# A halved Fourier transform in a transformer pair on one core, and twelve instead of four output-weight chunks loaded among the gate tiles

## The reference

```
sh1, sc1, g1, sh2, sc2, g2 = split(silu(c) @ w_mod + b_mod, 6)
h = rms_norm(x, norm_g[0]) * (1 + sc1) + sh1
hg = h.reshape(B, 256, 8, 256)                       # 8 groups of 256 features
y = real(fftn(hg, axes=(tokens, features in a group))).reshape(B, 256, 2048) @ fnet_w_out
x = x + g1 * rms_norm(y, norm_g[1])
x = x + g2 * rms_norm(relu2(modulate(rms_norm(x, norm_g[2]), sh2, sc2) @ w_mlp_in) @ w_mlp_out, norm_g[3])
```

## Time and profile before

| | |
|---|---|
| median of 3 runs | 2141.73 us (2141.72 to 2143.09) |
| the profiled execution | 2140.67 us, of which 2138.7 us is the span from the first to the last instruction |
| TensorE busy | 2096.8 us, 98% |
| VectorE busy | 1316.0 us, 62% |
| ScalarE busy | 985.5 us, 46% |
| mean granted TensorE clock | 0.997 |
| output product (f0 to f31) on TensorE | 172.69 to 264.92 us |
| start of the second half of the first MLP pair on TensorE | 321.24 us |

### The profile page before, as it was taken

How to read it: one execution, slowest core, us unless ns; L and a number is a source line. 1 busy time by engine, 2 the same in 40 slices (tenths; PEclk the granted TensorE clock), 3 DMA queues, 4 the chain that set the end, 5 groups by cost and what they waited for, 6 DMA issues and landing times.

```text
span 2138.7 us, 30220 instructions
## 1 busy us (share of the span) xinstructions
PE 2096.8 (98%) x11177; PEld 1764.5 (83%) x11177; DVE 1316.0 (62%) x1310; ACT 985.5 (46%) x1261; POOL 46.5 (2%) x71
## 2 busy tenths in 40 slices
PE   6899999999999999999999999999999999999999
PEld 3767878888888888887988888888888888888887
DVE  3878987656655655656767476555645655554553
ACT  4344355444344443434555567553434434343442
POOL 0010000000000000001100000000000000000000
PEclk9999999999999999999999999999999999999999
DMA  9999997677667667666665555566566656656654
GB/s 388 383 394 395 389 391 213 213 222 210 211 221 208 216 213 219 210 211 215 198 179 158 155 158 181 193 182 191 189 196 187 190 193 189 190 190 194 188 191 154
DMA packets 219374, 479.52 MB, mean 224 GB/s; under 512 B 14764, under 2 KB 15144, under 8 KB 218520
## 3 DMA queue, kind: packets, MB, share of 16 engines
q1 hardware_dynamic: 211956, 450.98, 65.1%
q0 software_dynamic: 6656, 26.21, 3.9%
q10 hardware_dynamic: 676, 1.14, 0.1%
HBM read 473.02 MB, written 5.25 MB: 224 GB/s over the span
## 4 chain that ended last, share of the span: by engine, by line
PE 89%; DVE 4%; DMA 3%; ACT 2%; issue 1%; SPq 1%; DVEq 0%; ACTq 0%
PE ps L537 46%; PE ps L499 21%; PE ps L504 11%; DVE acc L1552 2%; DMA raw<-in_w_mod_dram 1%; PE ps L521 1%; PE ps L523 1%; PE ps L522 1%; DMA raw<-in_w_mem_kv_dram 1%; PE ps L586 1%; PE ps L795 1%; PE ps L793 1%; PE ps L794 1%; PE ps L909 1%; PE ps L625 1%
## 5 line engine op out<-in xcount | busy, mean ns | idle before, releaser
L1527 DVE TENSOR_TENSOR wl<-raw,wh 128x1024 fp32r<-128x1024 f32 x684 | 808.2, 1222 | 314.1 <-ACT wh L1082 313.0
L1082 ACT ACTIVATE wh<-raw 128x1024 fp32r<-128x1024 f32 x684 | 696.7, 1054 | 522.4 <-DMA raw<-in_w_down_dram 161.9
L499 PE MATMUL ps<-xt,wh 128*128 128x512 f32 x1984 | 623.4, 395 | 1.6 <-DVE xt L1766 0.8
L537 PE MATMUL ps<-wh,u 128*128 128x512 f32 x2176 | 584.7, 389 | 1.0 <-DVE u L2052 0.6
L537 PEld LDWEIGHTS ps<-wh,u 128*128 128x128 f32 x2176 | 407.4, 188 | 85.8 <-DVE u L2052 1.0
L504 PEld LDWEIGHTS ps<-xt,wl 128*128 128x128 f32 x1984 | 372.7, 188 | 88.0
L504 PE MATMUL ps<-xt,wl 128*128 128x256 f32 x1984 | 389.7, 278 | 0.0
L537 PE MATMUL ps<-wl,u 128*128 128x512 f32 x1088 | 335.2, 389 | 0.0
L499 PEld LDWEIGHTS ps<-xt,wh 128*128 128x128 f32 x1984 | 302.5, 189 | 4.0 <-issue 2.5
L537 PE MATMUL ps<-wh,xt 128*128 128x512 f32 x960 | 269.1, 394 | 4.1 <-DVE wl L1527 2.8
L537 PEld LDWEIGHTS ps<-wl,u 128*128 128x128 f32 x1088 | 204.2, 188 | 42.4
(11 more groups left out here) (298 smaller groups left out, 1383.2 us busy)
## 6 DMA issues: line engine op xcount, KB each, us to landing
raw<-in_w_mod_dram SPq DMA_DIRECT2D x144, 512.0 KB, 9.8
raw<-in_w_mlp_in_dram SPq DMA_DIRECT2D x128, 512.0 KB, 3.8
raw<-in_w_mlp_out_dram SPq DMA_DIRECT2D x128, 512.0 KB, 4.8
raw<-in_w_up_dram SPq DMA_DIRECT2D x128, 512.0 KB, 3.8
raw<-in_w_down_dram SPq DMA_DIRECT2D x128, 512.0 KB, 3.7
raw<-in_w_in_dram SPq DMA_DIRECT2D x96, 512.0 KB, 3.8
slot<-in_w_mod_dram POOLq DMA_DIRECT2D x32, 512.0 KB, 5.2
raw<-in_w_out_dram SPq DMA_DIRECT2D x32, 512.0 KB, 3.7
```

The source lines that it names most:

```text
L499: mm(ps[:, 4 * par + j, :], wh[:, at, t, j * P:(j + 1) * P], flat(xt[:, kt, :, :]), start=kt == 0, stop=kt == KT - 1, skip_group_check=True)
L537: last = mm(o, act[:, kt, z, half * P:(half + 1) * P], w, start=kt == 0 and n == 0, stop=kt == KT - 1 and n == 2, skip_group_check=True)
L1082: A(flat(wh[:, i, :, :]), tile_at(landed[0]), ACT.Copy).then_inc(sem("w_hi"), 1)
L1527: V.tensor_tensor(flat(low_at(s)), tile_at(s), flat(wh[:, i, :, :]).bitcast(F32), ALU.subtract).then_inc(sem("w_lo"), 1)
```

## The change

The token transform of real data is symmetric in frequency, so half of the frequencies suffice. `dft_tokens` now makes `NF + 1` = 130 columns of the cosine and as many of the sine part (260 in all), and 129 of each are kept. `dft_features(q)` takes two groups at once, with 2 x 129 columns of cosine and 2 x 127 of sine sums, into separate column ranges of a bank, in 24 matmuls for each pair and 96 in all. The parts are then joined: ScalarE copies the two edge frequencies and the sine sums to `praw` (`fm_parts`), VectorE writes the difference and, in reversed order, the sum (`fm_sum`), and `fm_hi` and `fm_lo` split a pair's 1024 elements. The first two pairs' operands are prepared ahead of the first feature matmul. `G1_ROWS_AT` puts the rows of g1 tiles 8, 12 and 16 behind pairs 1, 2 and 3; those of tiles 20 to 23 come after the last pair, ahead of f0, and those of tiles 24 to 27 after f3. VectorE sums tiles 6 and 7 after the third pair's operands.

`AHEAD` goes from 4 to 12. On SyncE, 20 g1 tiles are alone, the last twelve alternate with f0 to f11, f12 to f31 have an sc2 tile each behind them, and twelve sc2 tiles follow f31. VectorE makes the low parts of f0 to f11 without sc2 sums beside them and has twelve of these sums after f31. `gate_rows` moves from behind f4 to behind f9, and the two halves of the gate to f12 and f13, the first output block to f14. All the slots from g1 tile 21 on move with the order, since they are counted from it.

```diff
-AHEAD = 4
+AHEAD = 12
...
-                            last = mm(o, xn[:, z, half, d0:d0 + P], t[:, half, :], start=half == 0 and z == 0 and t is dfth,
+                            last = mm(o, xn[:, z, half, d0:d0 + P], freqs(t[:, half, :])[:, :, 0:NF + 1], start=half == 0 and z == 0 and t is dfth,
...
+            def dft_features(q):
+                pe.wait_ge(sem("p_lo"), q + 1)
+                if q >= 2:
+                    pe.wait_ge(sem("fm_sum"), q - 1)
                 for dq in range(2):
+                    o = ps[:, pair_bank(q) + dq, :]
                     for kt in range(2):
                         for part in range(2):
                             lhs = slice(part * S + dq * P, part * S + (dq + 1) * P)
+                            cols = slice(2 * NF, 2 * S) if part else slice(0, 2 * NF)
+                            start = kt == 0 and part == 0
+                            mm(o[:, cols], dfth[:, kt, lhs], pdft[:, q % 2, kt, 0, cols], start=start, stop=False, skip_group_check=True)
+                            mm(o[:, cols], dftl[:, kt, lhs], pdft[:, q % 2, kt, 0, cols], start=False, stop=False, skip_group_check=True)
+                            last = mm(o[:, cols], dfth[:, kt, lhs], pdft[:, q % 2, kt, 1, cols], start=False,
...
-            for g in range(8):
-                dft_features(g)
-                if g in G1_ROWS_AT:
-                    n = G1_ROWS_AT[g]
+            for q in range(PAIRS):
+                dft_features(q)
+                for n in G1_ROWS_AT[q]:
                     if n == KT:
                         pe.wait_ge(sem("tok_out"), 8)
                     mod_rows("g1", C_G1, n, 2 if n < KT else 4)
             pe.wait_ge(sem("rows_folded"), 5)
+            mod_rows("g1", C_G1, 20, 4)
...
                     N_chunk(G_FN + g, i, xt, False, *early(CH * (G_FN + g) + i), fn_bank(g))
-                    if (g, i) == (0, 4):
+                    if (g, i) == (0, 3):
+                        mod_rows("g1", C_G1, 24, 4)
+                    if (g, i) == (1, 1):
                         pe.wait_ge(sem("rows_folded"), 6)
                         pe.wait_ge(sem("mod_out"), 2)
                         gate_rows(0, (4, 5, 6, 7))
...
+            def fm_parts(q):
+                act.wait_ge(sem("dft_d"), q + 1)
+                A(fm(q)[:, :, :, 0:NF:NF - 1], even_sums(q, slice(0, NF, NF - 1)), ACT.Copy)
+                A(fmq(q), ps[:, pair_bank(q):pair_bank(q) + 2, 2 * NF:2 * S].rearrange("p d (g n) -> p g d n", g=2),
+                  ACT.Copy).then_inc(sem("fm_part"), 1)
+            def fm_hi(q):
+                act.wait_ge(sem("fm_sum"), q + 1)
+                A(turned_rows(q, 0), fm(q), ACT.Copy).then_inc(sem("fm_hi"), 1)
...
+            def fm_sum(q):
+                dve.wait_ge(sem("fm_part"), q + 1)
+                t = fm(q)
+                V.tensor_tensor(t[:, :, :, 1:NF - 1], even_sums(q, slice(1, NF - 1)), fmq(q), ALU.subtract)
+                V.tensor_tensor(t[:, :, :, S - 1:NF - 1:-1], even_sums(q, slice(1, NF - 1)), fmq(q),
+                                ALU.add).then_inc(sem("fm_sum"), 1)
...
-                    if g == 0 and i < AHEAD:
+                    if CH * g + i < AHEAD:
                         continue
                     lo_static(CH * G + i)
                     gemv("sc2", C_FN, CH * g + i - AHEAD, 1)
-                    if (g, i) in ((0, 6), (1, 1)):
-                        gate(0, (4, 6), 0, (g,))
-                    if g and i == 3:
+                    if (g, i) in ((1, 4), (1, 5)):
+                        gate(0, (4, 6), 0, (i - 4,))
+                    if g and i == (3 if g > 1 else 6):
                         y_block(g - 1)
...
-G1_ROWS_AT = {1: 8, 2: 12, 3: 16, 4: 20, 5: 24}
-G1_AT = [(6, 7), (), (), (), (), (), (), ()]
+G1_ROWS_AT = [(), (8,), (12,), (16,)]
+G1_AT = [(6, 7), (), (), ()]
```

More of the change, by code:

```diff
@@ L696, in dft_features @@
                             lhs = slice(part * S + dq * P, part * S + (dq + 1) * P)
-                            mv_ = slice(part * S, (part + 1) * S)
-                            start = dq == 0 and kt == 0 and part == 0
-                            mm(o, dfth[:, kt, lhs], pdft[:, g % 2, kt, 0, mv_], start=start, stop=False, skip_group_check=True)
-                            mm(o, dftl[:, kt, lhs], pdft[:, g % 2, kt, 0, mv_], start=False, stop=False, skip_group_check=True)
-                            last = mm(o, dfth[:, kt, lhs], pdft[:, g % 2, kt, 1, mv_], start=False,
+                            cols = slice(2 * NF, 2 * S) if part else slice(0, 2 * NF)
[3 more added lines that the diff above has]
+                            last = mm(o[:, cols], dfth[:, kt, lhs], pdft[:, q % 2, kt, 1, cols], start=False,
                                       stop=kt == 1 and part == 1, skip_group_check=True)
@@ L1184, in fm_hi @@
-            def fm_hi(g):
-                act.wait_ge(sem("dft_d"), g + 1)
-                A(xt[:, 2 * g:2 * g + 2, 0, :], ps[:, g % 2, :].rearrange("p (a b) -> p a b", a=2),
-                  ACT.Copy).then_inc(sem("fm_hi"), 1)
+                elif q >= 2:
+                    act.wait_ge(sem("dft_d"), q - 1)
+                for g in range(2):
+                    for dt in range(2):
+                        kt = 2 * (2 * q + g) + dt
+                        A(cos_part(q, dt, 0, g)[:, 1:NF], praw[:, dt, 0, 2 * q + g, 1:NF], ACT.Identity, scale=a1[:, kt:kt + 1])
+                        last = A(sin_part(q, dt, 0, g), praw[:, dt, 1, 2 * q + g, 1:NF - 1], ACT.Identity, scale=a1[:, kt:kt + 1])
@@ L1189, in _ @@
             p_hi(0)
-            for g in range(8):
-                if g < 7:
-                    p_hi(g + 1)
-                if g == 0:
+            p_hi(1)
+            for q in range(PAIRS):
+                if q == 0:
                     tok_out(7)
-                if g == 6:
+                fm_parts(q)
+                if q + 2 < PAIRS:
+                    p_hi(q + 2)
+                if q == PAIRS - 1:
                     hi_static(CH * G_FN)
-                fm_hi(g)
-                if g == 6:
+                fm_hi(q)
+                if q == PAIRS - 1:
@@ L1666, in p_lo_first @@
-            def p_lo_first(g):
-                if g:
-                    dve.wait_ge(sem("p_lo"), g)
-                for dt in range(2):
-                    kt = 2 * g + dt
-                    last = V.tensor_scalar(dc[:, dt:dt + 1], praw[:, dt, 0, g * S:g * S + 1], a1[:, kt:kt + 1],
-                                           s1[:, kt:kt + 1], ALU.mult, ALU.add)
-                link(last)
-                hi0, lo0 = (pdft[:, g % 2, :, z, 0:1].rearrange("p a b -> p (a b)") for z in range(2))
-                link(V.tensor_copy(hi0, dc[:, :]))
-                V.tensor_tensor(lo0, dc[:, :], hi0.bitcast(F32), ALU.subtract).then_inc(sem("p_lo"), 1)
@@ L1678, in p_lo, with p_lo_rest @@
[L1678 to L1680 removed]
+            def p_lo_rest(q):
+                dve.wait_ge(sem("p_hi"), q + 1)
+                for g in range(2):
+                    for dt in range(2):
+                        kt = 2 * (2 * q + g) + dt
+                        for out_, hi_, in_ in ((cos_part(q, dt, 1, g)[:, 1:NF], cos_part(q, dt, 0, g)[:, 1:NF], praw[:, dt, 0, 2 * q + g, 1:NF]),
+                                               (sin_part(q, dt, 1, g), sin_part(q, dt, 0, g), praw[:, dt, 1, 2 * q + g, 1:NF - 1])):
+                            V.scalar_tensor_tensor(out=out_, in0=in_, scalar=a1[:, kt:kt + 1], in1=hi_.bitcast(F32),
+                                                   op0=ALU.mult, op1=ALU.subtract)
@@ new lines, in p_lo_first @@
+            def p_lo_first(q):
+                if q:
+                    dve.wait_ge(sem("p_lo"), q)
+                for dt in range(2):
+                    for g in range(2):
+                        kt = 2 * (2 * q + g) + dt
+                        last = V.tensor_scalar(dc[:, 2 * dt + g:2 * dt + g + 1], praw[:, dt, 0, 2 * q + g, 0:1], a1[:, kt:kt + 1],
+                                               s1[:, kt:kt + 1], ALU.mult, ALU.add)
+                link(last)
+                hi0, lo0 = (pdft[:, q % 2, :, z, 0:2 * NF].rearrange("p d (g n) -> p d g n", g=2)[:, :, :, 0] for z in range(2))
+                dc0 = dc[:, :].rearrange("p (d g) -> p d g", d=2)
+                link(V.tensor_copy(hi0, dc0))
+                V.tensor_tensor(lo0, dc0, hi0.bitcast(F32), ALU.subtract).then_inc(sem("p_lo"), 1)
```

93 lines of the change are left out of this document (46 added, 47 removed).

## The result

The changed kernel takes 2157.39 us (median of 6 runs, 2154.74 to 2160.15); the kernel before took 2142.22 in the same comparison (6 runs, 2141.29 to 2143.09). The ratio is 1.0072, 95% interval 1.0061 to 1.0084: slower, by 15.2 us. The forecast was 2146.5 with a range to 2153.0, so the direction was right and the size three times too small.

A forecast was written before the change was run, and what follows sets the result against it. Before 321 us, loads were taken as the bound, the end following ml3's landing. Terms +2.5 (sh2 tile 0), +2.4 (ml0 gap), -0.8 (interference), +0.7 (clock) made +4.8 us: 2145.5, or 2146.5 as median; range 2142 to 2153.

The forecast's parts named there:

- Matmuls: Token and feature transforms: 10.6 and 11.5 us less TensorE time, none by itself on the DMA's path; 0.6 us taken.
- a narrow matmul is dear: Feature transform: 254-column matmuls take 0.38 us instead of 0.12, everything 6 to 7 us later, 2153 us; chance 0.10.
- The order of loads: Last gate tiles: tile 23 lands at 163.6, so the Fourier output product starts at 165.5 us, not 172.7.
- The output product: Fourier output product: its last weight chunk f31 is used at 258.3 us, 6.6 us earlier than before.
- I am wrong if: Signs against the forecast: f31 used before 256, ml3 landing before 300, or 254 columns costing more than 256.
- VectorE paces the product: Output product: a late second side gain holds f14's low part and stalls TensorE; at 4 us, 2150; chance 0.07.
- Where the look-ahead goes: After the product: sh2 tile 0's load waits for f31 instead of f27 and lands at 262.0, 2.5 us later.
- A new wait: First MLP chunk ml0 waits for sh2 tile 14's sum, landing 4.9 us later; dry gap +2.4, interference -0.8.
- Clock: TensorE idling among the features: four chances in ten of one more clock drop reaching the product, +0.7 us.
- ml3 sets the restart: First MLP pair: the whole kernel's end moves one for one with the landing of chunk ml3, forecast 4.1 us later.
- delays are hidden: Loads after the product: the ring's dry loads and ml0 gap are filled, ml3 unmoved, 2141 to 2143; chance 0.13.

The follow-up runs named there:

- the turned ring: The changed kernel with the ring of pieces turned by two slots, so the first MLP chunk overwrites sh2's tile 2 instead of tile 14: 2151.74 us, ratio 1.0045.
- the run with less load: The kernel before, with sh2's tiles 24 to 31 loading only 512 of their 1024 columns: 2142.53 us, ratio 1.0003.
- the early g1 sums: The changed kernel with the sums of g1's tiles 6 and 7 straight behind those of 4 and 5: 2154.92 us, ratio 1.0055.

## Why the prediction was wrong

**Matmuls, rival "a narrow matmul is dear".** Right. 254 and 258 columns follow each other every 0.12 us, and the features began at 138.4 (139.3 foretold). The rival is refuted.

**The order of loads: product at 165.5.** It was 170.1, 4.6 us late. Tile 23 landed at 167.4, not 163.6. I charged 0.4 us for tiles 6 and 7 being summed near 150; the queue moved 242 GB/s from 150 to 160 us, 166 under the 408 of before, which is 1660 KB or 4 us of it. The rows behind tile 23 then took 2.55 us instead of 1.92, at the lower clock.

**The output product: f31 at 258.3.** It was 265.7. Beside the 4.6 us, the product lasted 95.6 us instead of 92.8. The lower clock at its start (0.95 from 170 to 190 us) and two waits of together about 1.1 us are the part that I can name; the gate product waited 0.60 us for VectorE. Of the three signs after "I am wrong if", none came true: all three looked to the fast side or to the price of 254 columns, and none to an f31 that comes late.

**Rival "VectorE paces the product".** Its mechanism shows in the trace:

```profile
213.13 1.22 DVE L1770 TENSOR_TENSOR acc<-ps,slot 128x1024 f32<-128x1024 f32 x1 [4.49 <-DMA slot<-in_norm_g_dram]
```

VectorE stood idle for the second side gain for 4.49 us. But TensorE waited only 0.51 us for VectorE behind it (at 219.20), so the cover held, and its price of some 4 us did not come.

**Where the look-ahead goes.** This is the step that failed. Its mechanism was right: tile 0 was issued when f31 had been used. The term was +2.5 us, and measured it is +11.6. Of the 9.1 us between, 7.5 are f31's use at 265.8 instead of 258.3 (the two steps above), and 1.6 are the landing after 5.3 us instead of 3.7. The kernel before had shown 5.3 for this very load; the 3.2 us that the prediction worked out from the Trainium skill ("DMA: Bandwidth & Descriptors", on the anatomy of one DMA) were further off still. That section is about transfers issued from GpSimd. The loads here go out on SyncE's queue, and no run issues them from GpSimd. What the term left out is that the queue falls behind while twelve chunks stand in the ring: 4 us at 165 us, about 11.5 at 240. The sum, instead, let the early start of the product pay for the four chunks (11 us of TensorE's time) between f27 and f31.

**A new wait (ml0).** The mechanism was right and is shown: ml0 was issued behind the sum of tile 14, and the turned ring took the gap away. The dry gap was priced at 2.4 us and measured 5.7. Tile 14 landed 8.3 us later than foretold, and VectorE came to it 3.3 us later still, because the step above gave VectorE nothing to do behind f31: the twelve sums, 16 us at 1.34 each, had no term, though the earlier trace rows held the price of one. Tile 16's slot waited for TensorE's rows of tile 10 as well, which I had not listed. For ml0 to ml3, 15.1 us were allowed and 16.8 measured; the 0.8 taken off for interference did not come.

Put together, the sum of the load terms was +2.5 + 2.4 - 0.8 = 4.1 us for ml3, and the trace has 17.6. That the direction came out right was not luck, since both mechanisms are there; the size was missed in both terms, most of it in the first.

**Clock.** 0.7 us were allowed, for a drop that reaches the product. One came just at the product's start (0.95 from 170 to 190 us). A longer one, of 20.5 us at the lower level from 267.7 on, came where none was foretold; it lengthened `mod_sum`, but TensorE waited for a load behind it, and no run shows what the clock alone cost. The Trainium skill ("TensorE: Matmul & The Clock Gate", on what is happening) says that the throttled state is the default and activity releases it; the trace agrees, with 0.50 in the ten microseconds in which TensorE was busy for 2.80.

**ml3 sets the restart.** Right. ml3 landed at 315.35, 17.6 us later, beside a restart 17.75 later, and the distance between the two is 23.5 to 24.4 us in all fourteen traces. No run moves ml3 alone, but the run with less load leaves only what lies behind ml3 to change, and nothing moved.

**The rival "delays are hidden".** Refuted. Its reasoning would have needed a full queue, and the queue was at its emptiest where the delays arose.

What stays open: why the product lasts 3 us longer than foretold; how much of the queue's 11 us comes from slots that are parked and how much from VectorE's late sums near 150 us, since no run fills the hole at 170 us with twelve ahead; and whether the early g1 sums are worth their 2.5 us.

## What to carry to other kernels

Follow the stream of loads and not the engine with the longest wait: TensorE's idle time before `mod_sum` went from 11.46 to 17.36 us and the restart moved by 0.4. Write down, for one late load, when the same place in the order lands before and after; here that alone gave two thirds of the loss. Loads fetched far ahead occupy slots until they are used; a ring full of waiting pieces loads little else, and here the stream fell 11 us behind for a product that began 2.6 us sooner. When an order of loads is changed, list for each engine the work that now comes *after* the point where it used to finish, and price it from the trace: twelve tiles moved behind the last chunk are twelve loads, but also twelve sums on VectorE, and a later load may wait for a sum behind them. If a ring's length or starting point changes, write down which piece overwrites which, since one that lands on a late piece can stop the queue, and turning the ring costs nothing.

## What the runs showed that was not expected

TensorE's long wait was followed by a long stretch at the lower clock: after 11.46 us without work it ran the 32 one-column matmuls of `mod_sum` in 6.96 us instead of 3.63, and the granted clock was back at 2.4 GHz only 20.5 us after the drop. In the run without parked sums (halved, 4 ahead) the drop at the same place lasted 6.8 us and the same 32 took 4.14.

Saving work on an engine that is 98% busy bought nothing: with four ahead TensorE was busy 2078.0 us instead of 2096.8, and the ratio was 1.000. The 98% are an average; ahead of the product TensorE's saved time turned into waits (busy 6.87 of ten us from 150 to 160 us, 10.00 before).
